# A decoder step on one core: projections from raw x, with the root-mean-square factor applied behind the product

## The chip, the core and the metric

The kernel runs on one core of a Trainium2 chip. The metric is device time in microseconds (us), the median of several runs; lower is better. The core has five engines with queues of their own: TensorE (PE: matmuls, and PEld: its weight loads), VectorE (DVE), ScalarE (ACT), GpSimd (POOL) and SyncE (SP), which here only issues DMA. They wait for one another by semaphores. Several engines can issue DMAs.

## The reference

One layer of a hybrid decoder for a prompt of 1024 tokens and 8 sample tokens of width 1024, in fp32. What matters here is the head of the layer:

```
xn = x * rsqrt(mean(x * x, axis=-1) + EPS) * rms_mix_g      # one factor per token, one gain per column
p  = xn @ w_in                                              # (1032, 1024) @ (1024, 4104)
# four mLSTM heads and four retention heads, each with 128 columns of q, k, v and an output gate
gate = silu(p_g) (retention) or sigmoid(p_o) (mLSTM)
ig, lf = p_i + b_ig, log_sigmoid(p_f + b_fg)                # 4 + 4 gate columns
rq, rk = rotary(p_q, pos), rotary(p_k, pos)                 # retention heads
# chunks of 128 tokens: S = k q^T, times a decay matrix, times v, plus q times the running state
x = x + mix @ w_out
x = x + peer_ffn(rmsnorm(x))                                # 128 x 128 experts, the two long stages behind
```

Since the factor of a token multiplies its whole row of x, it can be applied before the product or to the rows of the product.

## The kernel before

**Stages.** The program is a mixer (`mixer_stages`: all heads, then the output product, until about 500 us) and two long stages over the experts (`up_phase` and `down_phase`), each a stream of matmuls. The change touches the first part of the mixer alone.

**Tiles.** Tokens are in nine tiles, eight of 128 and one of 8 sample tokens (t = NC), in the order `TOK = [0, 1, 2, 3, NC, 4, 5, 6, 7]`. A head's projection of a tile has 8 blocks of 128 input columns, with three matmuls each: x and w are split into a high part (rounded to the format of TensorE's fast fp32 path) and a low part, and hi*hi, hi*lo and lo*hi are added up in PSUM. `NTILE` = 8 heads x 9 tiles = 72 steps n; i is the place of the tile within its head. The first four heads are retention heads.

**x before the first head.** SP loads the nine row tiles into `mix` (tokens on partitions). ACT squares a tile with a running sum (`square`, L537), DVE adds EPS and divides (`root_mean`, L699), ACT takes the root, DVE inverts it (`root_inverse`, L703) and scales the tile (`x_scale`, L661). PE transposes it in 8 pieces into the PSUM tile `pb` (`x_turn`, L381), ACT copies pb to the high part `xh` (`x_high`, L546), DVE writes the low part (`x_low`, L675 and L676). In step n of the first head these run for tiles ahead: x_turn(n + 3), x_high(m + 2), x_low(n + 3), x_scale(n + 4).

**Weights.** SP loads blocks of a head's weights into a ring of four (`wr`); `w_high` (ACT, L563) and `w_low` (DVE, L694) split them with the gain as a scale. Block 4 of a head waits for w_low of block 0, and so on.

**The order of a step n.** It is written out by hand, engine by engine. PE: the first half of the projection of step n + 2, S = k q^T (L489, waits for ACT's copy `qkT`), the state product pU (L494, waits for DVE's `ka`), the other half, `turn(n + 1)` (L431: q and k of the next step transposed; waits for DVE's rotation), then pA (L500, L502). ACT in step m: gate (L600, Silu), the copy `pr` (L606), x_high(m + 2), in step 1 two sines for the sample tile's angles (L611), in step 5 the high part of the gate weights, and last qkT (L639). DVE in step n:

```
v.tensor_scalar(ka[:, :], kk, acol, ...)                 # L878
if hd == 0: x_low(n + 3)
dve.wait_ge(S["s_done"], p + 1)
v.scalar_tensor_tensor(sd[:, :], pS[:, 0:P], ...)        # L888
rotate(n + 1)                                            # L736 to L740, waits for pr of step n + 1
if hd == 0: x_scale(n + 4), and in step 0 angles(), in step 3 gates_weights()
```

then the state update C (L931) and the head's output with its statistics. Ahead of step 4 (the sample tile, i = 4) DVE adds two parts of its projection (`eight`, L685), on which ACT's gate of that step waits; in step 4 it builds `kbig` (L938) and updates eight states (L948) one by one, in turn with PE's products L512.

**The gate columns.** After steps 6, 7 and 8 PE multiplies a third of xh and xl (344 tokens) with the 36 gate columns (`gate_inputs`, L444 to L446); DVE adds the bias (L759, L760).

Of the kernel before, what the change touches and what calls it, by code (L numbers as in the profile page):

```python
# [27 lines left out]
H = 4  # L28
# [161 lines left out]
NTILE = NH * NT  # L190
Q = 32
# [6 lines left out]
def mixer_stages(nc, A, O, own, up, sb, ps, sem, keep, expire, ident, x2_dram, hs_dram, twin, late, first_query):  # L198
# [27 lines left out]
    with ExitStack() as st, nc.Block() as block:  # L226
# [52 lines left out]
        names = ("xn xt hi lo ss0 sq ms root0 rstd0 gain_in ident_in whi wlo w_free pj_done pj_out tr_done tr_out "  # L279
# [15 lines left out]

        def prompt(n):

            return NC * (n // NT) + TOK[n % NT]
# [5 lines left out]
        def _(sp):  # L304

            def x_load(m):
                t = TOK[m]
                sp.dma_start(mix[:rows(t), t, :], A["x"][t * P:t * P + rows(t), :]).then_inc(x_in[m], 16)
# [5 lines left out]
            for m in range(2):  # L314
                x_load(m)
            sp.dma_start(gain[:, :, :], A["gains"]).then_inc(S["gain_in"], 16)
            sp.dma_start(ident[:, :], A["ident"]).then_inc(S["ident_in"], 16)
            for kb in range(RAW):
                w_load(kb)
            for m in range(2, NT):  # L320
                x_load(m)
# [21 lines left out]
        def _(pool):  # L343
# [5 lines left out]
            pool.wait_ge(S["xt"], 4)  # L349
# [19 lines left out]
        def _(pe):  # L369
            mm, tp = nc.tensor.matmul, nc.tensor.transpose  # L370

            def x_turn(m):

                if m >= NT:
                    return
                t = TOK[m]
                pe.wait_ge(S["xn"], m + 1)
                if m:
                    pe.wait_ge(S["lo"], m)
                for k in range(ND):  # L380
                    last = tp(pb[:, k * P:k * P + rows(t)], mix[:rows(t), t, k * P:(k + 1) * P], ident[:rows(t), :rows(t)])  # L381
                last.then_inc(S["xt"], 1)
# [51 lines left out]
            def gate_inputs(c):  # L434
# [8 lines left out]
                for k in range(ND):  # L443
                    mm(dst, wifh[:, k, :], xh[:, k, s], start=(k == 0), stop=False)  # L444
                    mm(dst, wifh[:, k, :], xl(k)[:, s], start=False, stop=False)
                    last = mm(dst, wifl[:, k, :], xh[:, k, s], start=False, stop=(k == ND - 1))  # L446
# [26 lines left out]
            x_turn(0)  # L473
            x_turn(1)
            project(0, range(ND))
            x_turn(2)
            project(1, range(ND))
            turn(0)
            for n in range(NTILE):
# [3 lines left out]
                if hd == 0:  # L483
                    x_turn(n + 3)
# [44 lines left out]
        def _(act):  # L529
            ac = nc.scalar.activation  # L530

            def square(m):
                t, r = TOK[m], rows(TOK[m])
                act.wait_ge(x_in[m], 16)
                if m:
                    act.wait_ge(S["sq"], m)
                ac(gate[:r, 1, 0:NC, :].rearrange("p t n -> p (t n)"), mix[:r, t, :], ACT.Square,  # L537
                   accum_out=ss[:r, m:m + 1]).then_inc(S["sq"], 1)

            def x_high(m):  # L540

                if m >= NT:
                    return
                t, r = TOK[m], rows(TOK[m])
                act.wait_ge(S["xt"], m + 1)
                ac(xh[:, :, t * P:t * P + r], pb[:, :].rearrange("p (k n) -> p k n", k=ND)[:, :, 0:r],  # L546
                   ACT.Copy).then_inc(S["hi"], 1)
                if t == NC:
                    ac(xs[:, :, 0:NS], pb[:, :].rearrange("p (k n) -> p k n", k=ND)[:, :, 0:NS],
                       ACT.Copy).then_inc(S["xs_done"], 1)  # L550
# [19 lines left out]
            act.wait_ge(S["ss0"], 1)  # L570
            for m in range(2):
                square(m)
            act.wait_ge(S["ms"], 1)
            ac(rstd[:, 0:2], ss[:, 0:2], ACT.Sqrt).then_inc(S["root0"], 1)
# [3 lines left out]
            x_high(0)  # L578
            for m in range(2, NT):
                square(m)  # L580
            act.wait_ge(S["ms"], 2)
            ac(rstd[:, 2:NT], ss[:, 2:NT], ACT.Sqrt).then_inc(S["root0"], 1)
            x_high(1)
            for k in range(4, ND):
                w_high(0, k)
            for m in range(NTILE):
# [13 lines left out]
                ac(gate[:r, hd % 2, t, :], src[:r, 3 * P:4 * P], ACT.Silu if ret else ACT.Sigmoid)  # L600
# [5 lines left out]
                ac(pr[:r, m % 3, 0:3 * P], src[:r, 0:3 * P], ACT.Copy).then_inc(S["pj_out"], 1)  # L606
# [45 lines left out]
        def _(dve):  # L652
# [3 lines left out]
            def x_scale(m):  # L656

                if m >= NT:
                    return
                t, r = TOK[m], rows(TOK[m])  # L660
                v.tensor_scalar(mix[:r, t, :], mix[:r, t, :], rstd[:r, m:m + 1], None, ALU.mult).then_inc(S["xn"], 1)  # L661

            def x_low(m):
# [6 lines left out]
                pk = pb[:, :].rearrange("p (k n) -> p k n", k=ND)  # L670
                if t == NC:
                    dve.wait_ge(S["xs_done"], 2)
                    v.tensor_tensor(xs[:, :, Q:Q + NS], pk[:, :, 0:r], xs[:, :, 0:NS].bitcast(F32),
                                    ALU.subtract).then_inc(S["xs_done"], 1)
                v.tensor_tensor(xla[:, :, s], pk[:, 0:3, 0:r], xh[:, 0:3, s].bitcast(F32), ALU.subtract)  # L675
                v.tensor_tensor(xlb[:, :, s], pk[:, 3:ND, 0:r], xh[:, 3:ND, s].bitcast(F32),  # L676
# [20 lines left out]
            def root_mean(part, s):  # L697
                dve.wait_ge(S["sq"], s.stop)
                v.tensor_scalar(ss[:, s], ss[:, s], 1.0 / D, EPS, ALU.mult, ALU.add).then_inc(S["ms"], 1)  # L699
# [1489 lines left out]
```

## Time and profile before

| | |
|---|---|
| median of 3 runs | 3344.01 us (3339.24 to 3352.62) |
| the profiled execution | 3348.13 us, span 3346.0 us, mean granted clock 0.977 |
| PE, PEld busy | 3212.8 us (96%), 2839.5 us (85%) |
| DVE, ACT, POOL busy | 2470.3 (74%), 989.5 (30%), 738.4 us (22%) |
| x_turn, 0 to 400 us | 72 transposes, 11.6 us busy |
| square, L537 | 9 of 1.056 us, and 9 of 0.187 us that read the sum |
| x_high, L546 | 8 of 1.02 us (128 tokens), 1 of 0.198 us |
| pr, gate, qkT (L606, L600, L639) | 0.49, 0.27, 0.38 us |
| w_high, w_low (L563, L694) | 0.72, 0.74 us |

The profile's times are of one execution, counted from its first instruction. Busy times of PE are modelled: matmuls overlap their neighbours, so that what holds the queue is the distance from start to start. The clock is TensorE's granted clock as a share of 2.4 GHz; 0.50 is 1.2 GHz.

### The profile page before, as it was taken

What the parts mean: (1) busy time and instruction counts of PE and PEld (TensorE: products, weight loads), DVE (VectorE), ACT (ScalarE), POOL (GpSimd) and SP (SyncE); (2) the same over time, 40 slices, a digit from 0 to 9 for tenths busy, and PEclk for the clock granted to TensorE, in tenths of its full rate; (3) what the DMA queues carried; (4) which work ended last, traced back from release to release, by engine and by line L of the source; (5) the groups of instructions that cost most, each with busy time, mean ns of one, the idle gap of its engine ahead of it and who ended that gap; (6) DMA issues with size and microseconds to landing.
All of it is one profiled execution on the core that took longest, in us unless ns stands there. A gap on an engine that the chain in (4) does not pass through costs nothing. (4 is left out here: it accounts for less than half of the span.)

```text
span 3346.0 us, 51054 instructions
## 1 busy us (share of the span) xinstructions
PE 3212.8 (96%) x18076; PEld 2839.5 (85%) x18076; DVE 2470.3 (74%) x5191; ACT 989.5 (30%) x1481; POOL 738.4 (22%) x565
## 2 busy tenths in 40 slices
PE   7999999799999898999999999998999999999998
PEld 5777777588999898999999999987888888888886
DVE  5565555435999779999677777747888888888884
ACT  3223332222112123444322222222333334333332
POOL 0000000000000000000166666644333333433320
PEclk9999999799999999999999999999999999999999
DMA  3111210222221123666799999979999999999982
GB/s 108 39 46 46 65 40 27 85 86 100 70 70 58 56 89 117 210 214 203 275 397 383 377 359 358 361 273 406 390 356 349 353 357 376 382 358 352 358 307 113
DMA packets 323282, 750.05 MB, mean 224 GB/s; under 512 B 22184, under 2 KB 153772, under 8 KB 322016
## 3 DMA queue, kind: packets, MB, share of 16 engines
q1 hardware_dynamic: 144896, 408.29, 33.2%
q0 software_dynamic: 79776, 290.00, 22.9%
q10 hardware_dynamic: 98496, 50.33, 5.2%
q8 instruction: 60, 0.98, 0.1%
q14 instruction: 54, 0.44, 0.0%
HBM read 633.59 MB, written 114.95 MB: 224 GB/s over the span
## 5 line engine op out<-in xcount | busy, mean ns | idle before, releaser
L1208 PE MATMUL u_p<-hn_hi,u_hi 128*128 128x384 f32 x2048 | 699.7, 342 | 18.7 <-DVE u_lo L1197 12.8
L1209 PE MATMUL u_p<-hn_lo,u_hi 128*128 128x384 f32 x2048 | 693.2, 338 | 0.0
L1210 PE MATMUL u_p<-hn_hi,u_lo 128*128 128x384 f32 x2048 | 693.1, 338 | 0.0
L1703 POOL DMA_INDIRECT s_ring<-in_peer_u,row_idx x264 | 333.0, 1261 | 1213.9 <-DVE row_idx L1796 1005.0
L1899 POOL DMA_INDIRECT y_ring<-in_peer_v,row_idx x240 | 356.0, 1483 | 610.1 <-DVE yt L2038 555.8
L1944 PE MATMUL y_p<-v_hi,w_hi 128*128 128x512 f32 x1536 | 474.5, 390 | 12.0 <-DVE w_lo L2029 10.5
L1946 PE MATMUL y_p<-v_lo,w_hi 128*128 128x512 f32 x1536 | 473.7, 390 | 0.0
L1949 PE MATMUL y_p<-v_hi,w_lo 128*128 128x512 f32 x1536 | 473.7, 390 | 0.0
L1208 PEld LDWEIGHTS u_p<-hn_hi,u_hi 128*128 128x128 f32 x2048 | 386.4, 189 | 21.0 <-DVE u_lo L1197 13.4
L1210 PEld LDWEIGHTS u_p<-hn_hi,u_lo 128*128 128x128 f32 x2048 | 386.5, 189 | 0.0
L1209 PEld LDWEIGHTS u_p<-hn_lo,u_hi 128*128 128x128 f32 x2048 | 386.3, 189 | 0.0
L1217 ACT ACTIVATE act_tile<-u_p 128x384 f32<-128x384 f32 x256 | 125.8, 491 | 860.5 <-PE u_p L1210 860.5
L1944 PEld LDWEIGHTS y_p<-v_hi,w_hi 128*128 128x128 f32 x1536 | 288.8, 188 | 73.3 <-DVE v_lo L2025 7.8
L1804 DVE CUSTOM_DVE_ANT_0 s_junk<-s_ring,s_hr 128x1024 f32<-128x1024 f32 x256 | 313.2, 1224 | 42.1 <-DMA s_ring<-in_peer_u,row_idx 15.6
L1946 PEld LDWEIGHTS y_p<-v_lo,w_hi 128*128 128x128 f32 x1536 | 289.0, 188 | 60.2
L1949 PEld LDWEIGHTS y_p<-v_hi,w_lo 128*128 128x128 f32 x1536 | 288.9, 188 | 60.1
L2038 DVE SCALAR_TENSOR_TENSOR yt<-y_ring,row_weight,yt 128x1024 f32<-128x1024 f32 x240 | 307.5, 1281 | 24.0 <-DMA y_ring<-in_peer_v,row_idx 7.0
L1197 DVE TENSOR_TENSOR u_lo<-u_raw,u_hi 128x1024 fp32r<-128x1024 f32 x128 | 156.2, 1221 | 173.7 <-ACT u_hi L1193 173.7
L1970 ACT ACTIVATE v_hi<-late 128x1024 fp32r<-128x1024 f32 x128 | 129.0, 1056 | 335.8 <-PE y_p L1949 333.3
L410 PE MATMUL pp<-late_r,xn_hi 128*128 128x512 f32 x512 | 221.3, 432 | 4.3 <-DVE late_r L694 3.8
L1970 ACT ACTIVATE v_hi<-down_raw 128x1024 fp32r<-128x1024 f32 x128 | 128.6, 1052 | 327.1 <-PE y_p L1949 327.1
L2025 DVE TENSOR_TENSOR v_lo<-down_raw,v_hi 128x1024 fp32r<-128x1024 f32 x128 | 151.0, 1221 | 89.1 <-ACT v_hi L1970 89.1
(346 smaller groups left out, 4853.3 us busy)
## 6 DMA issues: line engine op xcount, KB each, us to landing
u_raw<-in_peer_ut SPq DMA_DIRECT2D x128, 512.0 KB, 7.5
late<-in_peer_v SPq DMA_DIRECT2D x64, 1024.0 KB, 7.2
down_raw<-in_peer_v SPq DMA_DIRECT2D x64, 1024.0 KB, 7.0
act_scratch<-act_tile SPq DMA_DIRECT2D x128, 384.0 KB, 5.5
gate_scratch<-gbuf ACTq DMA_DIRECT2D x6, 4096.0 KB, 16.4
gate_scratch<-late ACTq DMA_DIRECT2D x6, 4096.0 KB, 17.8
late<-act_scratch SPq DMA_DIRECT2D x64, 384.0 KB, 8.4
late<-gate_scratch SPq DMA_DIRECT2D x64, 384.0 KB, 9.9
```

Source lines behind the costliest of these rows:

```text
L410: mm(dst, xh[:, k, tok], wh[:, k, :], start=(k == 0), stop=False)
L1208: mm(b, uh[:, s, k, :], hn_hi[:, k, t], start=(k == 0), stop=False)
L1209: mm(b, uh[:, s, k, :], hn_lo[:, k, t], start=False, stop=False)
L1210: last = mm(b, ul[:, s, k, :], hn_hi[:, k, t], start=False, stop=(k == ND - 1))
L1703: nc.gpsimd.indirect_dma_start(out=ring[:, s, :], out_offset=None, in_=src, in_offset=bass.IndirectOffsetOnAxis(ap=idx[:, column:column + ...
L1804: v.tensor_tensor_reduce(junk[:, :], ring[:, n % RING, :], h, 1.0, 0.0, ALU.mult, ALU.add, dots[:, n:n + 1]).then_inc(dot_done, 1)
L1899: nc.gpsimd.indirect_dma_start(out=ring[:, n % RING, :], out_offset=None, in_=A["peer_v"], in_offset=bass.IndirectOffsetOnAxis(ap=idx[:, N ...
L1944: mm(py[t][i][:, :], wh[:, s, e, tok], vh[:, s, e, i * 512:(i + 1) * 512], start=a, stop=False)
L1946: mm(py[t][i][:, :], wh[:, s, e, tok], vl[:, s, e, i * 512:(i + 1) * 512], start=False, stop=False)
L1949: done = mm(py[t][i][:, :], wl[:, s, e, tok], vh[:, s, e, i * 512:(i + 1) * 512], start=False, stop=z)
L1970: ac(vh[:, s, e, :], slot[r].v[:, e, :], ACT.Copy).then_inc(vhi_done, 1)
L2038: v.scalar_tensor_tensor(yt[:, t, :], ring[:, n, :], wt[:, bass.ds(column, 1)], yt[:, t, :], ALU.mult, ALU.add).then_inc(add_done, 1)
```

## The change

x comes in twice. A copy laid out by column (`xt`: for each tile, input column within the block on partitions, then block, then token; `xt8` for the sample tokens) is loaded into `mix` in place of the rows, so that x_high and x_low read raw x from SBUF (`turned`) and PE has no x_turn; x_scale is gone too. The rows are loaded once more, by ACT's own DMA queue, into two spare buffers (`row`: the space of `dm0` and of the second half of `gate`), and squared in place there, tile by tile within the steps. The factors come in three batches (tiles 0 and 1, 2 and 3, the rest) and are applied by ACT as the scale of the gate's and pr's copies, for all 72 steps. For the gate columns, PE multiplies the factors, broadcast over four rows, with the identity into the free half of `pb`, and DVE multiplies before it adds the bias. SP loads the first weights ahead of x tile 1 and the identity; the gate constants wait for all nine squares, since w_if shares a row buffer.

```diff
+BATCH = [(0, 2), (2, 4), (4, NT)]
+        row = [dm0[:, 0:D], gate[:, 1].rearrange("p t n -> p (t n)")[:, 0:D]]
+        def turned(t):
+            return mix[:, t, 0:ND * rows(t)].rearrange("p (k n) -> p k n", k=ND)
...
-                sp.dma_start(mix[:rows(t), t, :], A["x"][t * P:t * P + rows(t), :]).then_inc(x_in[m], 16)
+                sp.dma_start(turned(t), A["xt"][t] if t < NC else A["xt8"]).then_inc(x_in[m], 16)
...
-                if kb == ND:
+                if kb == ND + 2:
+                    sp.wait_ge(S["sq"], NT)
...
-            pool.wait_ge(S["xt"], 4)
+            pool.wait_ge(S["hi"], 4)
...
-            def x_turn(m):
...
+                if c == 0:
+                    pe.wait_ge(S["rstd0"], len(BATCH))
+                for i, t in enumerate(TOK):
+                    lo, hi = max(s.start, t * P), min(s.stop, t * P + rows(t))
+                    if lo < hi:
+                        last = mm(pb[:H, 512 + lo - s.start:512 + hi - s.start],
+                                  rstd[:rows(t), i:i + 1].broadcast_to([rows(t), H]),
+                                  ident[:rows(t), lo - t * P:hi - t * P], start=True, stop=True)
...
+            def row_load(m):
+                if m >= 2:
+                    act.wait_ge(S["sq"], m - 1)
+                nc.scalar.dma_start(row[m % 2][:r, :], A["x"][t * P:t * P + r, :]).then_inc(row_in[m % 2], 16)
+            def square(m):
+                act.wait_ge(row_in[m % 2], 16 * (m // 2 + 1))
+                ac(row[m % 2][:r, :], row[m % 2][:r, :], ACT.Square, accum_out=ss[:r, m:m + 1]).then_inc(S["sq"], 1)
+                row_load(m + 2)
+            def root(part):
+                act.wait_ge(S["ms"], part + 1)
+                ac(rstd[:, a:b], ss[:, a:b], ACT.Sqrt).then_inc(S["root0"], 1)
             def x_high(m):
-                act.wait_ge(S["xt"], m + 1)
+                act.wait_ge(x_in[m], 16)
+                ac(xh[:, :, t * P:t * P + r], turned(t), ACT.Copy).then_inc(S["hi"], 1)
...
+                if hd == 0:
+                    act.wait_ge(S["rstd0"], sum(m >= a for a, b in BATCH))
+                   scale=rstd[:r, i:i + 1])
...
+                ac(pr[:r, m % 3, 0:3 * P], src[:r, 0:3 * P], ACT.Copy, scale=rstd[:r, i:i + 1]).then_inc(S["pj_out"], 1)
...
+                if m < 2:
+                    square(2 * m + 4)
+                    square(2 * m + 5)
+                elif m == 2:
+                    square(8)
+                    root(2)
...
-                v.tensor_scalar(ig[:, s], pb[:H, 0:TC], bif[:, 0:1], None, ALU.add).then_inc(S["pre_out"], 1)
-                v.tensor_scalar(zf[:, s], pb[Q:Q + H, 0:TC], bif[:, 1:2], None, ALU.add).then_inc(S["pre_out"], 1)
+                ch.link(v.tensor_copy(zf[:, s], pb[:H, 512:512 + TC]))
+                v.tensor_tensor(ig[:, s], pb[:H, 0:TC], zf[:, s], ALU.mult).then_inc(S["pre_out"], 1)
+                v.tensor_tensor(zf[:, s], pb[Q:Q + H, 0:TC], zf[:, s], ALU.mult).then_inc(S["pre_out"], 1)
+                ch.mark(v.tensor_scalar(ig[:, s], ig[:, s], bif[:, 0:1], None, ALU.add))
+                ch.mark(v.tensor_scalar(zf[:, s], zf[:, s], bif[:, 1:2], None, ALU.add))
...
                     if hd == 0:
-                        x_scale(n + 4)
+                        elif i == 1:
+                            root_mean(2)
+                        elif i == 2:
+                            root_inverse(2)
```

ACT, from the copy of step 0 to that of step 2, before (gate and pr are the step's copies, xn_hi is x_high, cosin the sines, qkT the copy that ends a step):

```order
L606 ACTIVATE pr<-pp0 128x384
L546 ACTIVATE xn_hi<-pb 128x8x128 [waits h_xt]
L639 ACTIVATE qkT<-pt 128x256 [waits h_tr_done]
L600 ACTIVATE gate<-pp1 128x128 [waits h_pj_done]
L606 ACTIVATE pr<-pp1 128x384
L546 ACTIVATE xn_hi<-pb 128x8x128 [waits h_xt]
L611 ACTIVATE cosin<-shared 8x64 [waits h_ang_done]
L612 ACTIVATE cosin<-shared 8x64
L639 ACTIVATE qkT<-pt 128x256 [waits h_tr_done]
L600 ACTIVATE gate<-pp0 128x128 [waits h_pj_done]
```

The same place in the changed kernel, from the copy of step 0 to the sines of step 1 (dm0 and gate with ss are the squares in the two row buffers):

```order
L618 ACTIVATE pr<-pp0,rstd 128x384
L557 ACTIVATE xn_hi<-mix 128x8x128 [waits h_x_in2]
L651 ACTIVATE qkT<-pt 128x256 [waits h_tr_done]
L543 ACTIVATE dm0,ss<-dm0 8x1024 [waits h_row_in0]
L538 DMA dm0<-in_x 128x1024 [waits h_sq]
L543 ACTIVATE gate,ss<-gate 128x1024 [waits h_row_in1]
L538 DMA gate<-in_x 128x1024 [waits h_sq]
L611 ACTIVATE gate<-pp1,rstd 128x128 [waits h_rstd0,h_pj_done]
L618 ACTIVATE pr<-pp1,rstd 128x384
L557 ACTIVATE xn_hi<-mix 128x8x128 [waits h_x_in3]
L623 ACTIVATE cosin<-shared 8x64 [waits h_ang_done]
```

Two squares and two DMA issues stand between the copy qkT of a step and the gate, pr and x_high of the next. DVE in step 0 of the changed kernel, from `ka` on (rot and rot_m1, rot_m2 are the rotation's):

```order
L891 TENSOR_SCALAR ka<-rot,rcol 128x128 [waits h_rot_done]
L686 TENSOR_TENSOR xn_lo_a_r<-mix,xn_hi 128x3x128 [waits h_hi]
L687 TENSOR_TENSOR xn_lo_b_r<-mix,xn_hi 128x5x128
L901 SCALAR_TENSOR_TENSOR sd<-pS,dmat 128x128 [waits h_s_done]
L749 TENSOR_TENSOR rot_m1<-pr,cosin 128x256 [waits h_pj_out]
```

Its order is that of before, x_low ahead of sd and the rotation; only what x_low reads has changed, from `pb` to `mix`.

## Rows read from the trace of the kernel before

**Rows 1.** Which engines the chain that ended last names, page part 4.

```profile
PE 31%; DVE 0%; DMA 0%; issue 0%; ACT 0%; POOL 0%; DVEq 0%; ACTq 0%
```

**Rows 2.** Waits of 38 to 70 us: total, times, longest.

```profile
DVE xn_lo_a_r L675 <- ACT xn_hi L546: 6.7, 2, 5.2
...
ACT xn_hi L546 <- PE pb L381: 1.2, 2, 0.8
PE pt L431 <- DVE rot L740: 0.8, 1, 0.8
```

**Rows 3.** Stretches between turns: length, busy PE PEld DVE ACT POOL, clock, DMA, GB/s.

```profile
38.29:45.42 7.13, 7.13 (x40) 6.00 (x38) 3.97 (x12) 1.90 (x4) 1.08 (x1) 1.00 0.25 74
45.42:52.68 7.26, 7.26 (x42) 5.99 (x40) 5.78 (x24) 1.66 (x8) 0.00 (x0) 1.00 0.00 1
52.68:58.36 5.68, 5.68 (x36) 3.67 (x35) 4.62 (x15) 1.96 (x4) 0.00 (x0) 1.00 0.00 0
58.36:66.89 8.53, 7.74 (x43) 6.33 (x43) 6.39 (x18) 2.01 (x4) 0.00 (x0) 1.00 0.01 2
66.89:73.33 6.44, 4.51 (x25) 3.63 (x26) 4.05 (x11) 2.09 (x5) 0.00 (x0) 1.00 0.00 0
```

**Rows 4.** Timeline, head: start, length, engine, line, operation, [idle before].

```profile
13.69 12.85 SPq L311 DMA_DIRECT2D wp_raw<-in_w_heads  x5
...
15.50 1.06 ACT L537 ACTIVATE gate<-mix 128x1024 f32<-128x1024 f32 x1
...
16.74 1.06 ACT L537 ACTIVATE gate<-mix 8x1024 f32<-8x1024 f32 x1
...
25.45 2.73 DVE L694 SCALAR_TENSOR_TENSOR late_r<-wp_raw,gain,late_r 128x512 fp32r<-128x512 f32 x4
...
26.24 0.80 PE L410 MATMUL pp<-late_r,xn_hi 128*128 128x512 f32 x1 [3.08 <-DVE late_r L694]
...
31.53 1.37 PE L381 MATMUL pb<-ident,mix 128*128 128x128 f32 x8
```

**Rows 5.** Busy time and clock of five stretches, columns as in Rows 3.

```profile
0.00:21.40 21.40, 6.35 (x23) 5.43 (x24) 8.29 (x20) 15.12 (x23) 0.20 (x4) 1.00 0.92 336
...
26.00:32.00 6.00, 5.76 (x15) 4.50 (x16) 2.84 (x5) 2.17 (x5) 0.00 (x0) 0.50 0.50 141
...
70.00:76.00 6.00, 3.58 (x17) 2.26 (x16) 5.52 (x14) 0.00 (x0) 0.00 (x0) 1.00 0.00 0
76.00:91.00 15.00, 13.26 (x47) 8.36 (x47) 4.60 (x15) 1.11 (x4) 0.90 (x1) 0.54 0.00 0
...
284.00:286.00 2.00, 0.58 (x4) 0.35 (x2) 1.86 (x7) 0.00 (x0) 0.00 (x0) 1.00 0.00 0
```

**Rows 6.** Timeline of the tiles 0 and 1, columns as in Rows 4.

```profile
38.51 1.04 PE L381 MATMUL pb<-ident,mix 128*128 128x128 f32 x8
...
39.30 0.48 PE L410 MATMUL pp<-late_r,xn_hi 128*128 128x512 f32 x1
...
39.58 1.03 ACT L546 ACTIVATE xn_hi<-pb 128x1024 fp32r<-128x1024 f32 x1
...
42.18 0.38 PE L489 MATMUL pS<-qkT 128*128 128x128 f32 x2
...
42.60 0.29 DVE L888 SCALAR_TENSOR_TENSOR sd<-pS,dmat 128x128 f32<-128x128 f32 x1 [0.67 <-PE pS L489]
...
44.01 0.74 DVE L661 TENSOR_SCALAR mix<-mix,rstd 8x1024 f32<-8x1024 f32 x1
...
47.36 0.21 DVE L720 TENSOR_SCALAR shared<-shared 8x128 f32<-8x128 f32 x1
...
47.91 0.36 ACT L639 ACTIVATE qkT<-pt 128x256 f32<-128x256 f32 x1
```

**Rows 7.** Timeline of ACT at a change of function tables.

```profile
127.33 1.28 ACT L600 ACT_TABLE_LOAD   x1
128.63 0.28 ACT L600 ACTIVATE gate<-pp 128x128 f32<-128x128 f32 x1
```

More of the change, by code:

```diff
@@ L312, in w_load @@
                              ).then_inc(w_in[kb % RAW], 16)
-            for m in range(2):
-                x_load(m)
+            x_load(0)
             sp.dma_start(gain[:, :, :], A["gains"]).then_inc(S["gain_in"], 16)
-            sp.dma_start(ident[:, :], A["ident"]).then_inc(S["ident_in"], 16)
             for kb in range(RAW):
                 w_load(kb)
+            x_load(1)
+            sp.dma_start(ident[:, :], A["ident"]).then_inc(S["ident_in"], 16)
             for m in range(2, NT):
@@ L370, in _ @@
             mm, tp = nc.tensor.matmul, nc.tensor.transpose
-            def x_turn(m):
[L374 to L382, printed above, removed]
             def project(m, blocks):
@@ L568, in head_root @@
                 ac(mv[:, :, 1], mv[:, :, 1], ACT.Sqrt).then_inc(S["root_done"], 1)
[L570 to L574, printed above, removed]
+            row_load(0)
+            row_load(1)
+            x_high(0)
             act.wait_ge(S["gain_in"], 16)
@@ L577, in _ @@
                 w_high(0, k)
[L578 to L582, printed above, removed]
+            act.wait_ge(S["ss0"], 1)
+            square(0)
+            square(1)
             x_high(1)
+            root(0)
             for k in range(4, ND):
                 w_high(0, k)
+            square(2)
+            square(3)
+            root(1)
             for m in range(NTILE):
@@ L597, in _ @@
                     act.wait_ge(S["preset"], 1)
+                if hd == 0:
+                    act.wait_ge(S["rstd0"], sum(m >= a for a, b in BATCH))
                 if hd >= 2 and i == 0:
                     act.wait_ge(S["heads_done"], hd - 1)
-                ac(gate[:r, hd % 2, t, :], src[:r, 3 * P:4 * P], ACT.Silu if ret else ACT.Sigmoid)
+                ac(gate[:r, hd % 2, t, :], src[:r, 3 * P:4 * P], ACT.Silu if ret else ACT.Sigmoid,
+                   scale=rstd[:r, i:i + 1])
                 if m >= 3:
@@ L654, in _ @@
             ch = Chain(dve, S["chain"])
[L656 to L661, printed above, removed]
             def x_low(m):
@@ L836, in _ @@
             v.memset(ss[:, :], 1.0).then_inc(S["ss0"], 1)
-            root_mean(0, slice(0, 2))
+            x_low(0)
+            for k in range(4):
+                w_low(0, k)
+            root_mean(0)
+            x_low(1)
+            root_inverse(0)
+            v.memset(pr[:, :, :], 1.0).then_inc(S["preset"], 1)
+            for k in range(4, ND):
+                w_low(0, k)
+            root_mean(1)
+            root_inverse(1)
             ch.mark(v.memset(qm[:, :, :], 0.0))
@@ L845, in _ @@
             ch.link(v.memset(gate[:, :, NC, :], 1.0))
-            root_inverse(0, slice(0, 2))
-            x_scale(0)
-            x_scale(1)
-            v.memset(pr[:, :, :], 1.0).then_inc(S["preset"], 1)
-            for k in range(4):
-                w_low(0, k)
-            x_low(0)
-            root_mean(1, slice(2, NT))
-            root_inverse(1, slice(2, NT))
-            x_scale(2)
-            x_low(1)
-            for k in range(4, ND):
-                w_low(0, k)
-            x_scale(3)
             dve.wait_ge(S["ret_in"], 16 * 7)
```

53 lines of the change are left out of this document (24 added, 29 removed).

## The prediction, on record before the result

> **What bounds the kernel now.** I read the page's chain that ended last first. It is followed back only through the last third of the program, and there all but TensorE round to 0% of the span [rows 1]; the page's first part has PE busy 96% of the whole span. So the whole program is a queue of TensorE work, and what the change does in the mixer's first 130 us is worth what it does to TensorE's arrival at the end of them. Nothing later is touched but the scales in two ACT copies per tile. The second view was the waits of 38 to 70 us, the first retention head's first tiles [rows 2]. The reader should see there that PE hardly waits (0.8 us, for the rotation), while DVE waits 6.7 us for ACT's x_high (line 546). The third was busy time in the stretches between two `turn`s (PE's L431) [rows 3]: in the first three PE is busy 7.13 of 7.13, 7.26 of 7.26 and 5.68 of 5.68 us. There TensorE's own queue is the limit; in the fourth it has 0.79 us idle and in the fifth 1.9.
>
> **What goes from TensorE.** All nine x_turn. Eight transposes of 1.04 us let the next matmul start 0.79 us after them (38.51 to 39.30) [rows 6]; those of 31.53 take 1.37 and so hold the queue for 1.1 [rows 4]; the 8-row tile I put at 0.6, and the last, at half clock, at 1.5. Counted alone: x_turn(2) to (8), 1.1 + 4 x 0.8 + 0.6 + 1.5 = 6.4 us, and (0), (1) stand in the head. Off DVE go nine x_scale of 0.74 us (44.01) [rows 6]. Were PE's queue all that mattered, this would be the gain. It isn't, because x_high, x_low and the rotation form a second chain that runs ACT, DVE, PE, and the change puts work into it.
>
> **The head.** Before, PE projects tile 0 with blocks 0 to 3, then stands 3.08 us until w_low(4), at 26.24 [rows 4], since ACT squared seven tiles ahead of w_high(4). After, ACT does w_high(4) early, but the loads decide. Up to 21.4 us the DMA engines are 92% busy at 336 GB/s, 7.2 MB, with w blocks 4 to 7 the last to be issued (from 13.69) [rows 4, 5]. The changed kernel issues four row loads of 512 KB (tiles 0 to 3) from ACT's queue within the same time: 2.1 MB more, which at 365 GB/s (336 over the share of 0.92) is 5.7 us. w block 7 then lands at 27.1 and block 4, 0.75 MB or 2.1 us earlier, at 25.0. One w_high and one w_low (2.73/4 = 0.7 us each [rows 4]) bring PE to 26.4, 0.1 after before. From there both orders run 12 matmuls at half clock; the new one has no x_turn(2) behind: +0.1 - 1.1 = -1.0 us. Bounds: -5 us (the row loads delay nothing, block 4 at 21.4, PE at 22) and +2 (the two queues disturb each other). I take -1.0, since the rows have the engines full.
> The Trainium skill (DMA: Bandwidth & Descriptors, "Issuing engines are not separate DMA queues") says that DMAs started by different engines run on the same 16 DMA engines and interleave; by it the row loads take their bytes from the x and w loads, and -1.0 is what it gives; were each queue to have its own engines, -5. The trace of before has one queue at work in the head, so it neither confirms nor denies it.
>
> **Tiles 0 to 3: the new chain.** The order of DVE puts x_low(n+3) ahead of sd(n) and rotate(n+1), and PE's turn(n+1) waits for that rotation. x_low needs x_high, which ACT does one tile later behind that tile's gate and pr. The change puts squares ahead of these: (4), (5) after tile 0's qkT, (6), (7) after tile 1's, (8) and a square root after tile 2's. A square costs 1.24 us from start to start, 8 rows or 128 (15.50, 16.74) [rows 4]. Three of those slots also issue a DMA from ACT's queue; the trace has no such issue there, the nearest row is SP's (12.85 us for five, mostly waiting); bounds 0 and 0.5 us, I take 0.4. The new per-partition scales of gate and pr: w_high, 0.71 us for 512 columns with such a scale, against pr's 0.49 for 384 without, leaves some 0.1 us for each, 0 to 0.2.
> - turn(0) to turn(1), 7.13 before. x_high(3) ended 2.3 us after turn(0) (39.58 + 1.03 - 38.29) [rows 3, 6]. Now + 2 x 1.24 + 0.8 + 0.2 = 5.8. x_low 1.3 (from 40.61 to 42.60 less the 0.67 of waiting), sd and rotation 1.7 (42.60 to 0.3 after the x_scale's start), 0.1 to PE: 8.9. PE alone would need 7.13 - 0.8 = 6.3, so it idles 2.6. **+1.8**.
> - turn(1) to turn(2), 7.26 before. After the rotation DVE computes the angles (from the x_scale's end, 44.7, to 47.57: 2.9 us), on which ACT's sines wait; sines 0.3 (qkT began at 47.91), qkT 0.4, two squares and one issue 2.9, gate and pr 0.9, the small x_high with xs 0.55, x_low 0.6, sd and rotation 1.7, handovers 0.1: 10.3. **+3.0**.
> - turn(2) to turn(3), 5.68 before. Handover and qkT 0.8, square 1.24, table load for Sqrt 1.28 [rows 7], sqrt 0.3, load back for Silu 1.28, gate and pr 0.9, x_high 1.0, x_low 1.3, sd and rotation 1.7: 9.8. **+4.1**. The cover that hid such ACT work at 127 us (no x_high behind it) is not there.
> - turn(3) to turn(4): the chain over `eight` set it already (0.79 idle); same links, +0.2.
> Behind a table load the Trainium skill (ScalarE: Activation LUTs, "What ACT_TABLE_LOAD costs") puts a drain of some 1.38 us, 2.66 in all. Here the load of 127.33 is followed by its gate at 128.63, 1.30 later [rows 7]: no such drain, the trace decides; with the page's figure the sum would be 2.8 higher.
>
> **Behind tile 3.** ACT's x_high(7) waited 0.8 for x_turn(7) [rows 2], and gates_weights, C and kbig, for which PE idles, stand behind it: -0.8. x_scale(8) leaves the front of the sample updates, where PE waits for DVE: up to -0.74, I take -0.5. x_turn(8) at half clock: -1.5. The gate rows get 11 products of rstd with the identity; an fp32 product of 128 columns is two records of together 0.38 us that overlap their neighbours (42.18) [rows 6], so some 0.2 us each, less for the narrow: +2.0 (0 to 4). DVE's three added operations per third are smaller than an x_scale of 0.74 and lie where PE has its 24 long gate products to do; I count nothing, without this cover up to 2 us a third. SP's new wait for all squares stands ahead of w_if and five w blocks; the squares end about 2 us after turn(2), gates_weights comes some 16 us later, the w blocks later still: nothing.
>
> **Sum.** -1.0 + 1.8 + 3.0 + 4.1 + 0.2 - 0.8 - 0.5 - 1.5 + 2.0 = +7.3 us. On top the clock. A stretch with PE busy 3.58 of 6 us was followed by half clock for some 14 us, 26 to 32 at half clock followed an idle of 3.08, and 284 to 286 with 0.58 of 2 left the clock whole [rows 5]. The new idles (2.6, 2.8, 4 us in three stretches) resemble the first two. A tile at half clock needs 6.2 x 2 = 12.5 us of PE against a chain of 9 to 10: +3 for each tile it covers. I take one of 0 to 3: +3. Total **+10**. The profiled execution took 3348.13 (span 3346.0), so 3358 for its like; it lies 4 us above the median of 3344.01, to which I add: **3354 us**.
>
> **Rivals.** I call within 0.5% (16.7 us) no change, about what a measurement of this kernel can tell: under 3327.3 is faster, over 3360.7 slower.
> (a) The chain bites and PE runs at half clock from turn(1) through tiles 1 to 3 and into the sample tile: +3 for each of three tiles, and +3 because the stretch of 76 to 91 starts sooner: +7 + 9 + 3 = +19, 3363. It passes 0.5% only when all three tiles and part of the last term come together. For it: PE idle 30 to 40% in a row of stretches. Against: each idle is 4 us or less, with 5 to 6 us of work between. 0.22.
> (b) The squares slip in beside other work (ACT is busy 1.7 to 2 of 6 to 7 us in these stretches [rows 3]): then -6.4 from the turns, +0.1 in the head, +2.0 and -1.3 as above: -5.6, 3338. Against: the order, x_low ahead of the rotation. 0.13.
> (c) (b), and the row loads delay nothing, and the half clocks of 26 to 32 and 76 to 91 go (3 and 5 us at most): -5.6 - 4 - 8 = -17.6, 3326. 0.06.
> (d) Main forecast, 3345 to 3362: 0.59.
> From these, with 0.01 of (b) below its edge: faster 0.07, no change 0.71, slower 0.22. The range, 3336 to 3366, takes in (b) and more than half of (a); the main case's own is 3345 to 3362.
>
> **What would show it.** Right: no pb<-ident,mix on PE; turn(0) about 1 us earlier; intervals between turns of about 9, 10, 10 and 8.7 us; DVE's long waits for ACT xn_hi, and PE's for the rotation of 2 to 4 us, in tiles 0 to 2; two table loads around the root of five columns; w block 4 landing at 24 to 26 us; the interval from 130 us to the end unchanged. Wrong: intervals of 6.3, 6.7 and 5 us (then (b)), or w block 4 at 21 us with no idle before it, or a clock at 1.00 in all of 38 to 91 us.

## The result, and the profile after

The changed kernel took 3356.22 us (median of 11 runs, 3351.55 to 3373.19), the kernel before beside it 3340.10 (11 runs, 3336.09 to 3354.84). The ratio is 1.0042, with a 95% interval of 1.0028 to 1.0057: slower by 0.4%, within the 0.5% that the prediction called no change, and 2 us from the 3354 forecast. The medians are 16.1 us apart, where +10 was forecast. The profiled execution took 3361.95 us, span 3360.2, mean granted clock 0.975, against 3348.13, 3346.0 and 0.977: 14.2 us more of span.

The chain of waits, first read, looks as in [rows 1]:

```profile
PE 31%; DVE 0%; DMA 0%; issue 0%; ACT 0%; POOL 0%; DVEq 0%; ACTq 0%
```

So the turns were compared next (`turn(n)` transposes tile n's rotated q and k, and is now L427). In us from the start:

| turn | 0 | 1 | 2 | 3 | 4 | 5 | 6 | 7 | 10 | 30 |
|---|---|---|---|---|---|---|---|---|---|---|
| before | 38.29 | 45.42 | 52.68 | 58.36 | 66.89 | 85.13 | 96.65 | 103.34 | 134.67 | 294.28 |
| after | 38.54 | 47.05 | 56.77 | 66.13 | 75.55 | 93.14 | 103.21 | 109.89 | 143.93 | 305.44 |
| later by | 0.25 | 1.63 | 4.09 | 7.77 | 8.66 | 8.01 | 6.56 | 6.55 | 9.26 | 11.16 |

The stretches between these turns, and those of the head and of the clock, to be held against [rows 3, 5] (columns as there: length, busy PE PEld DVE ACT POOL, clock, DMA share, GB/s):

```profile
38.54:47.05 8.51, 6.41 (x32) 5.01 (x30) 2.77 (x9) 4.35 (x8) 1.08 (x1) 1.00 0.47 141
47.05:56.77 9.72, 7.21 (x32) 5.26 (x33) 5.38 (x25) 4.12 (x12) 0.00 (x0) 1.00 0.29 96
56.77:66.13 9.36, 5.28 (x27) 2.84 (x27) 4.65 (x16) 5.98 (x9) 0.00 (x0) 1.00 0.18 52
66.13:75.55 9.42, 8.47 (x35) 6.82 (x35) 5.94 (x17) 2.24 (x4) 0.00 (x0) 0.82 0.00 0
0.00:21.40 21.40, 5.33 (x12) 3.80 (x12) 6.88 (x12) 9.84 (x13) 0.20 (x4) 1.00 0.93 350
26.00:32.00 6.00, 3.59 (x9) 2.85 (x10) 2.74 (x4) 4.53 (x7) 0.00 (x0) 0.50 0.46 140
```

In each of the first three PE was wholly busy before [rows 3]; now it is idle 2.1, 2.5 and 4.1 us, while ACT's busy time has gone from 1.90, 1.66 and 1.96 to 4.35, 4.12 and 5.98. The waits of 38 to 76 us name the chain of [rows 2], longer (engine, line, what it waited for, total, times, longest):

```profile
DVE xn_lo_a_r L686 <- ACT xn_hi L557: 10.7, 3, 6.4
...
PE pt L427 <- DVE rot L753: 8.4, 4, 3.0
...
DVE xs L684 <- ACT xs L560: 3.7, 1, 3.7
```

PE waited 8.4 us for the rotation instead of 0.8, and DVE 14.4 for the high copies of x instead of 6.7. ACT's timeline shows what stands ahead of one of these copies, then the step with the table loads (start, length, engine, line, operation):

```profile
38.95 0.38 ACT L651 ACTIVATE qkT<-pt 128x256 f32<-128x256 f32 x1 [3.00 <-PE pt L427]
39.23 1.04 ACT L543 ACTIVATE dm<-dm 8x1024 f32<-8x1024 f32 x1
40.18 0.19 ACT L543 ACTIVATION_READ_ACCUMULATOR dm<-dm 8x1 f32 x1
40.40 0.34 ACTq L538 DMA_DIRECT2D dm<-in_x  x1
40.78 1.06 ACT L543 ACTIVATE gate<-gate 128x1024 f32<-128x1024 f32 x1 [0.41 <-ACT dm L543]
...
41.96 0.33 ACTq L538 DMA_DIRECT2D gate<-in_x  x1
42.40 0.37 ACT L611 ACTIVATE gate<-pp,rstd 128x128 f32<-128x128 f32 x1 [0.47 <-ACT gate L543]
42.66 0.57 ACT L618 ACTIVATE pr<-pp,rstd 128x384 f32<-128x384 f32 x1
43.13 1.06 ACT L557 ACTIVATE xn_hi<-mix 128x1024 fp32r<-128x1024 f32 x1
...
58.66 1.28 ACT L549 ACT_TABLE_LOAD   x1
59.95 0.21 ACT L549 ACTIVATE rstd<-ss 128x5 f32<-128x5 f32 x1
60.18 1.28 ACT L611 ACT_TABLE_LOAD   x1
61.47 0.37 ACT L611 ACTIVATE gate<-pp,rstd 128x128 f32<-128x128 f32 x1
```

From the end of qkT to gate(1) are 3.1 us: two squares of 1.14 each (39.23 to 40.37, the read of the sum included) and 0.4 to 0.5 around each DMA issue. x_high(3) began at 39.58 before [rows 6] and begins at 43.13 now.

The head, from the timeline of all engines:

```profile
16.39 13.64 SPq L318 DMA_DIRECT2D wp_raw<-in_w_heads  x7
...
26.85 2.56 ACT L572 ACTIVATE late_r<-wp_raw,gain 128x512 fp32r<-128x512 f32 x4 [8.69 <-DMA wp_raw<-in_w_heads]
27.60 2.74 DVE L705 SCALAR_TENSOR_TENSOR late_r<-wp_raw,gain,late_r 128x512 fp32r<-128x512 f32 x4 [8.01 <-ACT late_r L572]
...
28.41 0.80 PE L406 MATMUL pp<-late_r,xn_hi 128*128 128x512 f32 x1 [9.69 <-DVE late_r L705]
```

SP issued weight block 4 at 16.39, not 13.69 as in [rows 4], and it landed at 26.8; PE stood 9.69 us for it instead of 3.08 and went on 2.2 us later than before. That turn(0) is only 0.25 late has two reasons. x_turn(2) is gone, which took 1.1 us in before (from 31.53 to the next matmul at 32.65). And the half clock ended at about 32 us in both kernels: before ran its 12 matmuls of blocks 4 to 7 at half clock in 5.3 us (26.24 to 31.53), after ran three of them at the full clock and needed 4.6 (28.41 to 32.96). The gate rows' new products (columns: count, then busy time and mean ns):

```profile
L448 PE MATMUL pb<-ident,rstd 128*4 128x128 f32 (+5 forms) x22 | 2.4, 244 | 0.0
```

### The profile page after: what moved, and what is told of

The parts are those of the page before. It is cut to its first block and busy times, and to the rows that moved or that the text cites. A ratio compares the mean times of both kernels' runs of the same rounds, so it can differ in the third digit from the quotient of the medians.

```text
span 3360.2 us, 50958 instructions
## 1 busy us (share of the span) xinstructions
PE 3213.0 (96%) x18026; PEld 2834.4 (84%) x18026; DVE 2467.9 (73%) x5193; ACT 1004.6 (30%) x1484; POOL 735.2 (22%) x565
```

## Experiments

Every time is told with the median of before from the same chip in brackets; those five medians lie between 3340.1 and 3346.4. Times of turns are of one profiled execution each.

**1. The squares one place earlier in the same step**, in front of the wait for turn(m+1) and so of qkT.

```
+                if m < 2:
+                    square(2 * m + 4)
+                    square(2 * m + 5)
+                elif m == 2:
+                    square(8)
                 act.wait_ge(S["tr_done"], m + 1)
...
```

> The changed kernel with the squares of tiles 4 to 8 moved ahead of the copy qkT of their step (ACT waits there for PE's turn, 3 to 6 us), the third root left behind it. Theory A (the squares stand between qkT and the next x_high, and x_low stands ahead of the rotation that PE's turn needs): the intervals between turns 0, 1 and 2 fall from 8.51 and 9.72 us to about 6.5 and 7.5; turn 2 to 3 from 9.36 to about 8, since the two table loads of the root stay; about 5 us of the 16 come back, 3351. Rival B (the added 0.1 us per scaled copy, the row loads in the DMA queues, or half clock lengthen the steps): intervals stay within 0.5 us, no gain.

The intervals between turns 0 to 4 were 6.24, 8.86, 8.31 and 8.80. The first is free of the squares (PE alone needs 6.3, as the prediction reckoned). The second, for which 7.5 was expected, is not: there ACT waits 5.6 us for DVE's angles before its sines, and the squares come behind these, at 46.7. Turn 4 was 5.0 us earlier than in after; the time was 3359.51 (3341.40), ratio 1.0041 (1.0027 to 1.0056). The mechanism shows in the turns; the expected gain of 5 us does not show in the time.

**2. No late squares.** This kernel leaves out the row loads and squares of tiles 4 to 8, so the factors of those tiles are wrong.

```
-                if m >= NT:
+                if m >= 4:
                     return
...
-                if m < 2:
-                    square(2 * m + 4)
-                    square(2 * m + 5)
-                elif m == 2:
-                    square(8)
+                if m == 2:
                     root(2)
```

> The changed kernel without the row loads and squares of tiles 4 to 8 (their factors are then wrong), the third root with its table loads kept. Theory A: intervals of about 6.5, 7.2 and 8 us between turns 0, 1, 2, 3. If these equal the ones of the kernel that moves the squares ahead of the copy, moving hides them wholly. Rival B: intervals stay.

Intervals 6.24, 6.46 and 8.29 against 8.51, 9.72 and 9.36: the squares with their DMA issues cost 2.3 us in step 0 and 3.3 in step 1. In the third only 1.1 went, about one square. What is left of it is the root's: both table loads of 1.28 us are still ahead of the gate, PE is busy 5.17 of the 8.29 us, and the clock is 1.00. Time 3354.84, one run.

**3. Weight blocks 4 to 7 issued ahead of the loads of x.**

```
+            for kb in range(RAW, ND):
+                sp.wait_ge(S["wlo"], kb - RAW + 1)
+                w_load(kb)
             for m in range(2, NT):
                 x_load(m)
...
```

> The changed kernel with SP's loads of weight blocks 4 to 7 ahead of those of x tiles 2 to 8 and the constants. Theory C (in the head PE waits for block 4, which stands in the queue behind 3.9 MB of x and constants, and the row loads take bandwidth too): block 4 lands at about 14 us in place of 26.8, but ACT does two squares and a root ahead of its w_high, so PE goes on at about 19.5; turn 0 at 30 to 33 us in place of 38.5, and the kernel 6 to 8 us faster than the changed one, 3349. Rival D (ACT's squares or x's landing limit the head as much): turn 0 within 2 us of 38.5.

turn(0) came at 33.53, 5.0 us earlier, but DVE's first rotation then waited for the constants, whose issues had moved back:

```profile
32.19 0.43 DVE L752 TENSOR_TENSOR rot_m<-pr,cosin 128x256 f32<-128x256 f32 x1 [5.65 <-DMA eye<-in_eye]
...
33.53 0.69 PE L430 MATMUL pt<-ident,rot 128*128 128x128 f32 x2 [5.74 <-DVE rot L756]
```

The chain behind it was that of after: turn 2 came 4.7 us earlier than there, turn 10 4.9. Time 3354.02 (3341.40), 1.0031 (1.0014 to 1.0047): this interval overlaps that of after, so the 6 to 8 us that were expected are not shown.

**4. Before, with five squares of a zeroed buffer in the places where the change puts them**, without the DMAs, table loads and scales.

```
+                if m < 3:
+                    for j in range(2 if m < 2 else 1):
...
+                        ac(dm0[:, 0:D], dm0[:, 0:D], ACT.Square, accum_out=sx[:, 2 * m + j:2 * m + j + 1]).then_inc(S["sx"], 1)
...
```

> The kernel before with five squares of a zeroed spare buffer (1024 columns each, results unused) put on ACT at the places where the changed kernel squares tiles 4 to 8; no root, no row loads, x_turn kept. Theory A: intervals between turns 0, 1, 2, 3 grow from 7.13, 7.26, 5.68 to about 8.3, 9.3 and 7, and the whole kernel by 4 to 6 us. Rival B: intervals within 0.3 us, no change.

Intervals 7.34, 9.35, 6.19 and 8.56 against 7.13, 7.26, 5.68 and 8.53: +0.2, +2.1, +0.5 and nothing, 2.7 us in all at turn 4. About 8.3, 9.3 and 7 were expected, so the first and the third fell short. In step 0 before had most of the time to spare that two squares take; what after adds there beyond them (issues, longer copies) is what crosses over: x_high(3) ends 4.48 us after turn(0) here and 5.65 in after, 1.17 apart, and so are the intervals of 7.34 and 8.51. Time 3347.31 (3341.40), 1.0009 (0.9994 to 1.0025).

**5. After, with each step's squares behind its high copy of x, and the root in step 3.**

```
                 if hd == 0:
                     x_high(m + 2)
+                if m < 2:
+                    square(2 * m + 4)
+                    square(2 * m + 5)
+                elif m == 2:
+                    square(8)
+                elif m == 3:
+                    root(2)
...
```

> The changed kernel with the squares of tiles 4 to 8 directly behind the x_high of their step (so also ahead of the sines), and the third root in step 3, where ACT waits 3 to 4 us for the sample tile's sum. Head as in the changed kernel. Theory A: all intervals are PE's own, about 6.2, 6.5, 5.2 us, and turn 3 to 4 about 8.6; turn 4 comes about 9.5 us earlier than in the changed kernel, and the whole is 3347, within a few us of the kernel before. Rival B (half clock lengthens the steps by itself, whatever ACT does): turn 4 within 3 us of the changed kernel's.

Intervals 6.25, 6.46, 5.52 and 8.80: the first three are now shorter than before's. In program order each pair of squares has moved ahead of the qkT of its step. So tiles 4 and 5 are squared before turn(0), where ACT waits for PE anyway, and between turn(0) and turn(1) those of tiles 6 and 7 stand behind x_high(3), which begins at 40.05, not at 43.13 as in after:

```profile
39.05 0.38 ACT L658 ACTIVATE qkT<-pt 128x256 f32<-128x256 f32 x1 [1.32 <-PE pt L427]
39.33 0.36 ACT L611 ACTIVATE gate<-pp,rstd 128x128 f32<-128x128 f32 x1
39.58 0.58 ACT L618 ACTIVATE pr<-pp,rstd 128x384 f32<-128x384 f32 x1
40.05 1.07 ACT L557 ACTIVATE xn_hi<-mix 128x1024 fp32r<-128x1024 f32 x1
41.00 1.07 ACT L543 ACTIVATE dm<-dm 128x1024 f32<-128x1024 f32 x1
...
42.56 1.06 ACT L543 ACTIVATE gate<-gate 128x1024 f32<-128x1024 f32 x1 [0.41 <-ACT dm L543]
```

Turn 4 came at 65.66, 9.9 us earlier than in after and 1.2 earlier than in before. Time 3348.11 (3346.36), 1.0011 (0.9998 to 1.0024). This is the clearest of the set: no work is taken out, and the whole delay of the first three intervals goes with the place of the squares and the root. It shows in the time too: the ratio of after to before was 1.0042 (1.0028 to 1.0057), and the two intervals do not overlap.

**6. Experiment 5 with the weights first, and the first squares behind w_high.** DVE's order follows ACT's.

```
...
+            x_high(1)
+            for k in range(4, ND):
+                w_high(0, k)
             act.wait_ge(S["ss0"], 1)
             square(0)
             square(1)
-            x_high(1)
             root(0)
-            for k in range(4, ND):
-                w_high(0, k)
...
```

> The same with a new head: SP loads weight blocks 4 to 7 ahead of x tiles 2 to 8, and ACT and DVE do blocks 4 to 7 ahead of the first squares and root. Theory C (only the order of loads and of ACT's work holds PE in the head): no idle of PE over 3 us from its first matmul at 10 to 13 us on; turn 0 at 28 to 30 us in place of 38.5 (33.5 with the loads alone in new order), turn 4 at 55 to 57, the whole 3337 to 3341: level with the kernel before. Rival D (DMA bandwidth holds the head: 9.4 MB by 26 us): turn 0 at 33 us or later, or x tile 2 late.

turn(0) at 34.62, turn 4 at 64.60, turn 10 at 134.48. The start gained 3.7 us on before and the next stretch of 9.2 (7.1 before) took more than half of it back. That is what rival D had (33 us or later), not the 28 to 30 of the theory. What held turn(0) is again a load, this time of rows for the squares:

```profile
27.11 1.06 ACT L546 ACTIVATE dm<-dm 128x1024 f32<-128x1024 f32 x1 [4.01 <-DMA dm<-in_x]
...
34.62 0.69 PE L430 MATMUL pt<-ident,rot 128*128 128x128 f32 x2 [8.65 <-DVE rot L757]
```

Time 3351.80 (3346.36), 1.0020 (1.0005 to 1.0035).

**7. Before with such a head**: weights first, its seven squares behind w_high, x_turn(2) behind the second projection. SP's wait and DVE's order follow.

```
...
             x_high(0)
+            x_high(1)
+            for k in range(4, ND):
+                w_high(0, k)
             for m in range(2, NT):
                 square(m)
...
```

> The kernel before with the same new order in the head: weight blocks 4 to 7 loaded and split ahead of x tiles 2 to 8 and of seven of the nine squares, x_turn of tile 2 behind the second projection. Theory C: turn 0 at about 32 us in place of 38.3, then the intervals of before; 3335, 5 us faster than before. It tells how much of the gain of the combined version belongs to the head's order and not to raw x. Rival D: turn 0 within 2 us of 38.3, since the squares then delay x_turn(2) and the first rotation.

turn(0) at 34.84, turn 1 at 45.38, where it stands in before (45.42). About 32 us and 5 us of gain were expected, and neither came. Time 3345.02 (3346.36), 1.0001 (0.9986 to 1.0017).

**8. Before again, one profile.**

> The kernel before once more, unchanged, for a second profile. If the half clocks behind 130 us are set by the program, they stand at the same places as in the first profile and the turns agree within 0.5 us up to 540 us. If they are a matter of chance at idles of about 1 to 2 us, the first stretches agree and some single half clock is there or gone, each worth 1.5 to 6 us.

Up to turn 14 it ran within 0.25 us of the first. From there single half-clock stretches come and go: 2.7 us ahead at turn 15, 4.3 behind at turn 42, 1.5 ahead at turn 60. Time 3344.99.

**9. A version meant to beat both**: the constants ahead of weight blocks 4 to 7, these ahead of x; squares 0 and 1 behind w_high; the others in pairs (the last alone) behind the high copies of steps 0 to 3; the second root in step 1, the third in step 3.

```
...
+            for kb in range(RAW, ND):
+                sp.wait_ge(S["wlo"], kb - RAW + 1)
+                w_load(kb)
+            for m in range(2, NT):
+                x_load(m)
...
+                if m == 1:
+                    root(1)
+                if m < 3:
+                    square(2 * m + 2)
+                    square(2 * m + 3)
+                elif m == 3:
+                    square(8)
+                    root(2)
...
```

> After with four moves together: the constants' loads (rotation, masks) issued ahead of weight blocks 4 to 7, these ahead of the loads of x for tiles 2 to 8; squares 0 and 1 behind x_high(1) and w_high(4..7); squares 2 to 7 in pairs in steps 0 to 2, and 8 in step 3, directly behind that step's high copy of x (so all but two squares have left the head); each root in a later step. My theory: the earlier heads lost their gain because the first rotation waited for constants and for squares 2 and 3; here neither stands ahead of it, so turn 0 comes at about 28 to 31 us (before 38.3), and as squares behind x_high cost no more than in the run with them there (turn 4 at 65.7 with turn 0 at 38.6, so 27.0 from 0 to 4, here up to 30 as every step has two), turn 4 stands at 56 to 61 (before 66.9) and turn 10 at 124 to 129 (before 134.7). Time 3333 to 3341 us if that lasts, against 3340 to 3346 for before. Rival: the transfers of the head, not the order, set the pace (x for tile 2 and the rows are then late): turn 1 at 44 to 45 and turn 4 at 64 to 66 as in the runs with the new head, time 3345 to 3352.

turn(0) came at 26.08, 12.2 us before that of before, with next to nothing to wait for (the rows are PE's and its weight loads'):

```profile
26.08 0.20 PEld L430 LDWEIGHTS pt<-ident,rot 128*128 128x128 f32 x2 [0.37 <-DVE rot L755]
26.08 0.44 PE L430 MATMUL pt<-ident,rot 128*128 128x128 f32 x2
```

Turn 4 at 60.70 (before 66.89) and turn 10 at 125.64 (134.67), 9.0 ahead. The profiled span was 3332.3. And yet: median 3340.09 (3342.42), ratio 0.9997 (0.9982 to 1.0011). Turns 4 and 10 came where they were expected, turn 0 even 2 us earlier. But turns 0 to 4 took 34.6 us (28.6 in before, up to 30 expected), so half of the lead was gone at turn 4; from there to turn 10 this profile has about 3 us at half clock and that of before about 14. The median lies at the upper end of the 3333 to 3341 expected, and 12 runs do not show it below that of before.

**10. After again, one profile.**

> The changed kernel a second time, without any edit. If what the profile of after showed is set by the program, turns 0 to 10 come within 0.3 us of the first profile (38.54, 47.05, 56.77, 66.13, 75.55, and 143.9 for turn 10). If the half-clock stretch of 392 to 407 us is chance, it is missing or elsewhere here, and turn 42 comes about 5.7 us earlier against turn 40 (25.6 us after it in the first profile, 19.9 in before). Time 3350 to 3364.

Turns 0 to 3 within 0.04 us; turn 4 at 74.96 and turn 10 at 144.83, 0.6 earlier and 0.9 later, both from half-clock stretches that moved. From turn 40 to turn 42 it took 24.0 us, so the stretch of 392 to 407 did return; that expectation fell. Time 3358.64.

**11. The version of experiment 9 again.**

> The same kernel as in the run with the constants first, which by its profile stood 9.0 us ahead of before at turn 10 (125.64 against 134.67) and ended 10.6 us ahead of the second profile of before, but whose 12 times had a median only 2 us below (3340.1 against 3342.4). My theory: the head's gain is real in every run (turn 0 at 26.1, turn 10 at 125.6 again, within 0.3 us) and some of the runs lose it again in one more half-clock stretch of about 12 us behind the head, so the times lie in two clusters (3334 to 3341 and 3348 to 3351) and the median comes between 3337 and 3347. Rival: the gain lasts and the first median was bad luck: median 3331 to 3336, ratio to before below 0.998.

Turn 0 at 26.89 and turn 10 at 129.61: 5.1 ahead of before, not 9.0. At turn 4 it was still 5.7 ahead (6.2 in the first profile); then the stretch of 69 to 84 us ran at a clock of 0.54, where the first profile has 0.72 over 75 to 81 us and the full clock around it. By turn 42 the lead was gone (1.2 behind), and the profiled span was 3349.6. Median 3344.10 (3343.46), ratio 0.9996 (0.9981 to 1.0012). The expected two clusters of times (3334 to 3341, 3348 to 3351) fell: four of these 12 runs lie between, at 3343.11 to 3346.52. The two rounds of 12 agree: this version isn't faster than before in a way that can be measured.

**12. Before a third time, one profile.**

> The kernel before a third time, without edit, to see which half-clock stretches return: the two profiles so far agree within 0.3 us to turn 14 (166.9, 166.6), the first has stretches at 594 to 606 and 510 to 534 that the second lacks, the second has one at 384 to 396 that the first lacks. By my theory (chance) a third profile has another selection of them, and its time lies within 3334 to 3353 accordingly; by the rival (the first profile was odd in one place only) it repeats the second.

It had neither the half-clock stretches of 510 to 534 and 594 to 606 us nor that of 384 to 396: a third selection. Time 3338.64, span 3336.5.

## Why the prediction came out right, and where it missed

**The new chain of ACT, DVE and PE (+1.8, +3.0, +4.1, +0.2).** Measured +1.38, +2.46, +3.68 and +0.89, 8.4 for a forecast of 9.1. Experiments 2 and 5 show the cause: with the late squares out, or behind the high copy, the first two intervals fall to 6.2 to 6.5; the third, with both table loads left ahead of the gate, is still 8.29 in experiment 2 and is 5.52 in experiment 5. The first three terms were 0.4 to 0.5 too large each; part of this is that gate, pr and qkT overlap their neighbours by some 0.1 us each (gate 42.40, pr 42.66, x_high 43.13 above). The fourth ran in part at half clock (0.82), which the prediction had in its clock term; in after's second profile, with 0.81, it was 8.80, +0.27. Rival (b), squares that slip in, fell in after. It is what happens once the squares stand elsewhere (6.25, 6.46 and 5.52 in experiment 5, against its 6.3, 6.7 and 5). Rival (a), half clock through tiles 1 to 3, fell too: of the four stretches three have a clock of 1.00.

**The head (-1.0).** Measured +0.25. The failing step is block 4's landing, put at 25.0 and measured at 26.8. Row loads do take their bytes from the others': in the first 21.4 us the engines were 93% busy at 350 GB/s (in before 92% at 336 [rows 5]), and by 30 us queue q10, ACT's, had moved 2.10 MB. That is also what the Trainium skill says (DMA: Bandwidth & Descriptors, "Issuing engines are not separate DMA queues"), and here the trace agrees. What the prediction left out is that SP, too, issued later: the constants' issues took 0.55 to 2.57 us each (0.34 to 0.70 in before), and block 4's came right behind the last of them, 2.7 us behind its former place. And its "12 matmuls at half clock" in both orders was wrong for after, as shown above, which gave 0.7 us back.

**Behind tile 3 (-0.8, -0.5, -1.5).** From turn 4 to 5 -0.65, from 5 to 6 -1.45, then 0.01: 2.1 of the 2.8. This size isn't firm, since it is read across a half-clock stretch: from turn 4 to turn 7 before took 36.5 us in its first profile, after 34.3 and, in its second, 35.8, and experiment 5, with about 3 us at half clock in place of 14, 30.9. (The fifth stretch of [rows 3] ends at a state product within the step, not at a turn as the prediction has it.)

**The gate rows (+2.0).** From turn 7 to 10, +0.87, +0.86 and +0.98, so +2.7. The new products are busy 2.4 us. The scales' 0.1 us per copy came as put (gate 0.27 to 0.37, pr 0.49 to 0.57) and hid from step 10 on: steps 10 to 14 took the same time to 0.02 us.

**The clock (+3) and the sum (+10).** Up to turn 10 the sum was +7.3 without the clock and +10 with it, and +9.3 came, with the clock's part in it. The other 4.9 us of the profiled difference lie behind it, where the change left nothing but two longer copies per tile; the prediction had that stretch unchanged. They come with half-clock stretches, and these are in part chance. In before the step around 379 us has an idle of 0.95 us and keeps its clock; in the second profile of the same kernel it has an idle of 0.94 and loses it; in after, with 0.94, too. Stretches around that place, first before (length, busy PE, clock, DMA share, GB/s):

```profile
379.00:384.00 5.00, 4.05 (x19) 1.00 0.00 2
384.00:396.00 12.00, 11.71 (x60) 1.00 0.11 45
```

Before again (experiment 8):

```profile
378.50:384.00 5.50, 4.56 (x19) 0.93 0.00 0
384.00:396.00 12.00, 11.99 (x37) 0.50 0.00 1
```

After:

```profile
388.50:393.00 4.50, 3.56 (x18) 1.00 0.00 0
393.00:407.00 14.00, 13.99 (x44) 0.53 0.00 0
```

60 matmuls in 12 us at the full clock, 37 at half. Reading the difference of 5.7 us between turns 40 and 42 off the first pair of profiles as an effect of the change would have been wrong: before's second profile takes 25.6 us for these two steps, its first 19.9. Its third has the idle of 0.94 and keeps the clock, 19.9 again.

How much of the 16 us is clock? I summed (1 - clock) x 3 us over all windows of 3 us of a trace (idle time counts too, so this is a size and no cost). Before, three profiles: 79, 69 and 64 us. After, two: 86 and 83. The means are 14 us apart; of it some 6.5 lie in the first 130 us, where the idles are, and the rest between 130 and 1200, where no instruction of PE was added behind step 10. The record of all runs says the same with more weight, since it has each one's span and mean clock. After's 11 runs have a mean of 80.6 us for span x (1 - clock) and 3275.8 for span x clock; the 90 runs of before beside the experiments have 69.6 and 3272.0. Of the 14.9 us between the mean spans, 11 are clock and 4 are not. So the prediction's +3 holds the sign of the clock's part and is too small for it. A full account isn't to be had: these 11 to 14 us and the 9.3 of turn 10 overlap in the first 130 us, and no experiment takes the half clocks away.

**What stays open.** A lead at turn 10 doesn't show in the time: 9.0 and 5.1 us in experiments 9 and 11, 4.0 in experiment 5, with ratios of 0.9997, 0.9996 and 1.0011; yet after's lag of 9.3 does show. The two profiles of experiment 9's kernel have 60 and 83 us by the sum above, spans of 3332.3 and 3349.6. Its 24 times run from 3333.6 to 3352.4, about as widely as those of before. The half-clock stretches behind 130 us take the lead back in some of the runs; why in as many as to leave the median where it was, the profiles don't show. By the same means over all runs, experiment 5 has 3269.0 us for span x clock and 77.5 for span x (1 - clock), before beside it 3270.9 and 71.5; the two rounds of experiment 9 have 3270.3 and 3270.4, with 70.4 and 71.3, before beside them 3271.9 and 3272.5, with 70.4 and 69.0. So a lead of 4 to 9 us at turn 10 leaves some 2 us at the full clock, and what the half clock takes is larger by 6, 0 and 2. Nor is such a lead all work: up to 130 us the sum above is 10 in before and 2 and 9 in the two profiles of experiment 9, so that most of the 9.0 can be half clock that was missing in that one execution. No run holds fixed where the clock falls, so it wasn't tested whether the start of the mixer decides it.

So the forecast is borne out by its mechanism up to turn 10, where +7.3 to +10 was reckoned and +9.3 came. That the total agrees to 2 us is luck in good part. The difference was forecast at +10 and measured at 16.1, too small mainly by the clock's term, which was put at +3 from one profile of before, itself one of a spread. It was added to a median of 3344.01 from 3 runs; beside the changed kernel, before had 3340.10 from 11.

## What to carry to other kernels

Taking work from the busiest engine gains nothing where the replacement is queued on another engine ahead of what the busiest one waits for: here nine transposes of x went from PE, and five squares and a root on an ACT that was busy 30% of the time cost 9 us of the first three intervals by their place alone (27.6 us against 18.2), and nothing that shows in them once the squares stood behind the high copy of x and the root a step later. Follow each edit's chain from the instruction it is queued in front of, and when a load is moved in the head, look for the next load that becomes last (weights, then constants, then rows). For effects below 0.5%, compare the times at which marks in the program are passed, in two profiles of each kernel, before a difference is put down to the change.

## What the runs showed of the hardware that was not expected

- Half-clock stretches are in part chance. The same program with the same idle of 0.94 or 0.95 us ran the next 12 us at a granted clock of 1.00 in two profiles and 0.50 in the third. The Trainium skill (TensorE: Matmul & The Clock Gate, Part 1) says that the watch on TensorE's activity runs free and isn't reset when a kernel starts; these three profiles fit that, and no run here isolates it.
- The time of a run follows its mean clock: after's 11 runs go from 0.978 at 3351.55 us to 0.972 at 3373.19, and experiment 9's two groups of times have 0.979 to 0.982 (3334 to 3341) and 0.976 to 0.978 (3348 to 3351).
- A DMA issued by ACT between its ACTIVATEs took 0.33 to 0.34 us in steps 0 and 1, and the next ACTIVATE begins 0.38 after the issue did, behind a gap of 0.41 in all.
- With ACT's row loads in flight, single small issues of SP took up to 2.57 us (rcol at 10.20). Before has 0.59 for the same one, and experiment 3, with the row loads but another order of SP's, 1.06.
